# Norm roots on one core: square root, turned columns, reciprocal and spreading replaced by the exponential of a logarithm, in place in PSUM

## What is computed

```python
def rms_norm(x, g):
    xf = x.astype(jnp.float32)
    y = xf * lax.rsqrt(jnp.mean(xf * xf, axis=-1, keepdims=True) + EPS)
    return (y * g.astype(jnp.float32)).astype(x.dtype)

def layer_norm(x, g, b):
    xf = x.astype(jnp.float32)
    mu = jnp.mean(xf, axis=-1, keepdims=True)
    var = jnp.mean(jnp.square(xf - mu), axis=-1, keepdims=True)
    y = (xf - mu) * lax.rsqrt(var + LN_EPS) * g.astype(jnp.float32) + b.astype(jnp.float32)
    return y.astype(x.dtype)
```

## Time and profile before

| | us |
|---|---|
| median of 3 runs | 3126.02 (3125.41 to 3126.05) |
| the profiled execution | 3123.1 |
| its span, first to last instruction | 3121.3 |
| PE busy in it | 2922.6 (94%) |
| DVE busy | 1522.6 (49%) |
| ACT busy | 1160.0 (37%), of it 53 table loads 68.0 |
| POOL busy | 1310.3 (42%) |

### The profile page before, as it was taken

The page is one execution under the profiler, slowest core; times in us unless marked ns, Lnnn a source line. Parts: engine busy times, 40 slices in busy tenths (PEclk is TensorE's granted clock), DMA queues, the critical chain, the costliest instruction groups (busy, mean ns, idle before and its releaser), DMA issues.

```text
span 3121.3 us, 40174 instructions
## 1 busy us (share of the span) xinstructions
PE 2922.6 (94%) x15552; PEld 2150.9 (69%) x15552; DVE 1522.6 (49%) x2324; ACT 1160.0 (37%) x1827; POOL 1310.3 (42%) x798
## 2 busy tenths in 40 slices
PE   6999999999999999999999999998889979979997
PEld 4666557888888788888978888684564238546533
DVE  4765645563231545343341111556675655477665
ACT  4434424122111423333252222424434653453465
POOL 3644334454443435353445555457531024764200
PEclk9999999999999999999999999999999999989998
DMA  5310213444322112121123333220258932114695
GB/s 228 108 34 14 85 57 121 149 142 149 133 98 67 55 48 87 43 81 61 55 100 101 99 96 95 68 81 28 76 190 320 381 147 82 54 50 184 256 383 202
DMA packets 85884, 375.12 MB, mean 120 GB/s; under 512 B 9408, under 2 KB 11968, under 8 KB 76608
## 3 DMA queue, kind: packets, MB, share of 16 engines
q1 hardware_dynamic: 68416, 310.41, 28.5%
q10 hardware_dynamic: 12672, 45.37, 3.7%
q0 software_dynamic: 4608, 16.78, 1.4%
HBM read 557.07 MB, written 29.36 MB: 188 GB/s over the span
## 4 chain that ended last, share of the span: by engine, by line
PE 78%; DVE 11%; DMA 3%; ACT 3%; issue 2%; POOL 1%; SPq 0%; DVEq 0%; ACTq 0%; POOLq 0%
PE PS L105 77%; DVE SCR L120 2%; DMA ALL<-in_moe 2%; DVE SM L135 1%; PE PS L108 1%; DMA BF<-in_ada 1%; DVE SCR L132 1%; DVE SCR L126 1%; DVE SM L120 1%; DVE XF L126 1%; ACT SCR L114 1%; ACT RT L114 1%; DVE RTX L126 1%; DVE RTX L117 0%; DVE SM L123 0%
## 5 line engine op out<-in xcount | busy, mean ns | idle before, releaser
L105 PE MATMUL PS<-RT,WH 128*128 128x512 f32 (+1 forms) x5696 | 1518.5, 369 | 34.4 <-ACT SCR L114 9.4
L105 PEld LDWEIGHTS PS<-RT,WH 128*128 128x128 f32 x5696 | 1030.8, 190 | 271.2 <-issue 31.7
L120 POOL TENSOR_TENSOR WL<-RAW,WH 128x1024 fp32r<-128x1024 f32 x284 | 703.0, 2478 | 765.7 <-ACT WH L114 765.5
L105 PE MATMUL PS<-RT,WL 128*128 128x512 f32 (+1 forms) x2848 | 926.0, 366 | 0.0
L105 PEld LDWEIGHTS PS<-RT,WL 128*128 128x128 f32 x2848 | 493.2, 191 | 56.8
L114 ACT ACTIVATE WH<-RAW 128x1024 fp32r<-128x1024 f32 x284 | 298.4, 1054 | 602.4 <-PE PS L105 533.6
L120 POOL TENSOR_TENSOR RT<-SCR,RT 128x512 fp32r<-128x512 f32 (+2 forms) x174 | 222.6, 1287 | 406.3 <-ACT RT L114 314.3
L120 DVE TENSOR_TENSOR SCR<-PS,SCR 128x512 f32<-128x512 f32 (+1 forms) x106 | 58.8, 571 | 483.9 <-PE PS L105 465.9
L105 PE MATMUL PS<-ALL,SCR 128*32 x576 | 268.2, 610 | 24.4 <-DVE SCR L120 13.8
L105 PE MATMUL PS<-RTX,SCR 128*32 128x512 f32 x1152 | 268.4, 617 | 0.0
L126 DVE SCALAR_TENSOR_TENSOR XF<-PS,SM,XF 128x512 f32<-128x512 f32 x240 | 149.7, 658 | 216.3 <-PE PS L105 215.7
(11 more groups left out here) (238 smaller groups left out, 3639.9 us busy)
## 6 DMA issues: line engine op xcount, KB each, us to landing
ALL<-in_moe SPq DMA_DIRECT2D x100, 2048.0 KB, 8.4
ALL<-in_moe SPq DMA_DIRECT2D x100, 1024.0 KB, 14.0
RAW<-in_ff SPq DMA_DIRECT2D x132, 512.0 KB, 3.6
BF<-in_ada SPq DMA_DIRECT2D x64, 512.0 KB, 4.7
RAW<-in_ret SPq DMA_DIRECT2D x64, 512.0 KB, 3.5
RAW<-in_win SPq DMA_DIRECT2D x28, 512.0 KB, 3.5
RTX<-in_ada SPq DMA_DIRECT2D x26, 512.0 KB, 4.8
XF<-placed_in ACTq DMA_DIRECT2D x24, 512.0 KB, 8.7
```

Source lines behind the costliest of these rows:

```text
L105: return NOTHING if self.e is None else self.e.matmul(o, w, x, start=first, stop=last)
L120: return NOTHING if self.e is None else self.e.tensor_tensor(*a)
```

## The change

Four things are done:

- `act_root` computes ln(mean + eps) and then exp(-0.5 * that), both from the mean's bank in PSUM into the same bank. With it go the square root in SBUF, the turning, the columns' reciprocal and the spreading on PE and DVE; `dve_norm` reads the mean's bank, waits for ACT in place of PE, and the bank is given back by the last `dve_norm` (k = 7), not by `act_root`.
- Each two-part norm takes four banks fewer from the ring, each one-part norm two fewer. At the start four takes named "passed" keep the numbering of what follows.
- The retention's norm does the same in `RR` (SBUF), without the DVE reciprocal.
- `act_table` names Ln where it named Sqrt. Other square roots (attention heads, filters, token norms) stay.

```diff
         def act_root(act, s, j, n, eps):
-            r = sq_ring.take(("rr", s, j))[:, 0:n]
-            for count in sq_ring.empty(("rr", s, j)):
-                act.wait_ge(*count)
+            o = bank.of(("mean", s, j))[:, 0:n]
             act.wait_ge(*pe_done.at(("mean", s, j)))
-            act.activation(r, bank.of(("mean", s, j))[:, 0:n], ACT.Sqrt, bias=eps).then_inc(*act_done.done(("rr", s, j)))
-            bank.give(("mean", s, j), act_done.now())
-
-        def dve_root(dve, s, j, n):
-            r = bank.of(("rt", s, j))[:, 0:n].rearrange("p (c t) -> p c t", t=P)[:, :, 0]
-            dve.wait_ge(*pe_done.at(("rt", s, j)))
-            dve.reciprocal(root_column(j, n), r).then_inc(*dve_done.done(("rr", s, j)))
-            bank.give(("rt", s, j), dve_done.now())
+            act.activation(o, o, ACT.Ln, bias=eps).then_inc(*act_done.done())
+            act.wait_ge(*act_done.now())
+            act.activation(o, o, ACT.Exp, scale=-0.5).then_inc(*act_done.done(("rr", s, j)))
...
         def dve_norm(dve, s, k, j, n, A, B, *counts):
...
-            r = bank.of(("rb", s, j))[:, 0:n]
-            dve.wait_ge(*pe_done.at(("rb", s, j)))
+            r = bank.of(("mean", s, j))[:, 0:n]
+            dve.wait_ge(*act_done.at(("rr", s, j)))
             dve.scalar_tensor_tensor(h, XS[j][:, k, :], A[:, k:k + 1], r, ALU.mult, ALU.mult).then_inc(
                 *dve_done.done(("h", s, k, j)))
             if k == 7:
-                bank.give(("rb", s, j), dve_done.now())
+                bank.give(("mean", s, j), dve_done.now())
...
         def rms_pe(pe, s, parts):
             for j, _, n in parts:
                 pe_mean(pe, s, j, n)
-            if s != "att":
-                pe_roots(pe, s, parts)
...
                 if m == 11:
                     rms_pe(pe, "att", XP)
-            pe_roots(pe, "att", XP)
+            for n in range(4):
+                take_bank(pe, ("passed", n))
+                bank.give(("passed", n))
...
                 act.wait_ge(*pe_done.at(("rvar", h)))
-                act.activation(RR, bank.of(("rvar", h)), ACT.Sqrt, bias=EPS6).then_inc(*act_done.done(("rroot", h)))
+                act.activation(RR, bank.of(("rvar", h)), ACT.Ln, bias=EPS6).then_inc(*act_done.done())
                 bank.give(("rvar", h), act_done.now())
+                act.wait_ge(*act_done.now())
+                act.activation(RR, RR, ACT.Exp, scale=-0.5).then_inc(*act_done.done(("rroot", h)))
...
                 dve.wait_ge(*act_done.at(("rroot", h)))
-                dve.reciprocal(RR, RR).then_inc(*dve_done.done())
-                own()
                 for e in range(4):
```

More of the change, by code:

```diff
@@ L573, in pe_mean @@
             sq_ring.give(("sq", s, 7, j), pe_done.now())
[L575 to L600, removed]
         h_ring = ring([scr(0), scr(1), scr(2), scr(3)])
@@ L685, in rms_dve @@
         def rms_dve(dve, s, parts, A, B, before):
-            for j, _, n in parts:
-                dve_root(dve, s, j, n)
             free_h(dve, before)
@@ L858, in dve_ada @@
                     dve_add(dve, "att", k, j, n)
-            for j, _, n in XP:
-                dve_root(dve, "att", j, n)
             for b in range(2):
@@ L1410, in act_att @@
                             act_fold(act, g, blk)
-            act_table(act, ACT.Sqrt)
+            act_table(act, ACT.Ln)
             for g, m in OUT_LATE:
@@ L2119, in pe_variance @@
                 sq_ring.give(("sq", s, k, 0), pe_done.now())
-            pe_roots(pe, s, [(0, 0, S)])
         def act_layer_norm(act, s, b, before):
-            act_table(act, ACT.Sqrt)
+            act_table(act, ACT.Ln)
             for k in range(8):
@@ L2136, in dve_layer_norm @@
             bank.give(("mu", s), dve_done.now())
-            dve_root(dve, s, 0, S)
             free_h(dve, before)
```

## The result

The changed kernel takes 3149.69 us (median of 4 runs, 3147.0 to 3152.16) against 3125.72 (3122.55 to 3126.05) for the kernel before, run beside it: ratio 1.0077, 95% interval 1.0064 to 1.0091. It is slower by 24.0 us, where 18.8 was forecast. The profiled execution took 3151.77, its span is 3149.3.

What follows compares the result with a forecast made beforehand. PE, 78% of the chain, was taken to bound the kernel, norms counting only where it waits. Terms 11.15 + 2.06 + 2.85 + 2.1 + 1.04 - 0.45 = +18.75 us on 3126.02 gave 3144.8, range 3135 to 3152.

Steps and rivals of the forecast that it cites:

- Start: First norm: PE waits for the last normalization because the means' banks are held; +12.25 less 1.1, sum +11.15 us.
- "ff0": Two-part feed-forward norm: chain of 5.99 us on ACT ahead of `act_norm` shifts PE's start by +2.06 us.
- "ret": Retention's two-part norm: `act_norm` +2.85 us later, plus 2.1 for PE restarting at half clock.
- the credit of 1.1 for the clock: Start: PE's slow restart was to lose 2.1 us instead of 3.2, so -1.1.
- give or take 1: Clock at "ff0" and other already slow restarts: drawn anew, zero net, within 1 us each.
- One-part norms: Four norms ("ff1", "ln0", "ln1" twice): chain 2.62 instead of 2.36 us, +0.26 each, +1.04 together.
- Head 3: Last retention head: first product at 1578.7 instead of 1579.15, -0.45 us, bounds -1.5 and +1.9.
- hidden: Load ahead of the attention heads' first root: covered by 2.33 us of ACT idle time; uncovered it would cost 1.28.
- A: Rival: the late start is made up because something other than PE bounds attention; +9.6, 3135.6 us; chance 0.08.
- B: Rival: not slower, loads between Ln and Exp don't hold ACT; +2.4, 3128.4 us; chance 0.04.
- C: Rival: a load after a root costs twice its row, over 14 loads; +18, 3162.8 us; chance 0.05.
- D: Rival: first norms start as before, POOL not catching DVE, clock kinder; 3141 to 3143 us; 0.80 together with the forecast.

Runs made afterwards that it cites:

- the second group of runs: The changed kernel run again unaltered, with more rounds, for a second trace and firmer median: 3153.13 us (4 runs).
- e12: Changed kernel with two unread one-column memsets added among DVE's first instructions: 3152.2 us (5 runs).
- e10: Changed kernel with the two places of the first norm's roots put back in the ring of the squares' tiles: 3149.14 us (4 runs).
- e11: Kernel before with one more place taken in the ring of the squares' tiles behind the first norm: 3126.28 us (10 runs).
- e2: Kernel before with only the start's two mean banks given back late, by the last normalization: 3134.66 us (10 runs), ratio 1.0029.
- e1: Changed kernel with the four passed banks taken ahead of the start's means: 3140.67 us (4 runs), ratio 1.0044.
- e7: Changed kernel with 24 unread transposes behind the means of every RMS norm but the first: 3148.26 us (5 runs).
- e8: Changed kernel with passed banks ahead of the means, logarithms ahead of exponentials, 24 unread transposes, and the squares' ring as before: 3130.29 us (10 runs), ratio 1.0014.

## Why the prediction was right or wrong, step by step

- **Direction and mechanism** were right: slower, PE's wait at each norm, three loads in a row ahead of `act_norm`, the largest part of the loss a bank held at the start (8 to 10 of the 25 us). The Trainium skill, "ScalarE: Activation LUTs", section "What ACT_TABLE_LOAD costs", has a load of 1283 ns, which the trace repeats, and a drain of 1380 ns with it, which it doesn't: Ln ends at 32.43, the load begins at 32.45, Exp at 33.75. The size is another matter: by the table of stretches the forecast of 18.75 was 4.2 short. The start was 1.3 too small, "ff0" 2.6, and the three stretches that held only small terms or none 1.9 together; "ret" was 1.5 too large. That the time still fell inside the range is in part the luck of this one error against the others, and the second group of runs lies 1.1 us outside it.
- **Start, forecast +12.25 - 1.1 = +11.15.** First norm forecast at 41.5 and PE at 54.85; e12 has PE at 54.75 and e10 at 54.51. The wait was exact, the credit of 1.1 for the clock was mis-sized: from PE's first projection matmul to the mark at 112.34 it is 69.0 to 69.8 us with the old norms and 68.3 to 69.3 with the new, 0.5 in the mean. And one thing was missed. The means may run slowly, which the old norms hide but for 0.7 us and the new ones don't (56.85): 2.1 more, in two of four traces (I take the slow means for PE at half clock, which their lengths suggest, 1.22 and 1.06 as under a granted 0.50 ahead of "ff0", and the clock column doesn't show). Stretch by stretch: +12.4.
- **"ff0", forecast +2.06, measured +4.6.** The chain that was added up holds: Ln to `act_norm` is 5.91 (forecast 5.99). Set stretch by stretch, the 4.6 are 1.5 from the mark to the root, 2.4 from the root to PE's restart and 0.7 behind it. The 1.5 are what the sum had at nothing: DVE's addition caught beside POOL. The 2.4 are 7.62 us against 5.65 in two of the five old-norm traces and 4.87 in the other three; the forecast was read from one of the two, where slow means already delay the old `act_norm` (3.93 us behind the root instead of 3.14), so it came out as 2.06. The 0.7 are the clock, which was counted as even: it falls behind the restart in each of the four traces of the new norms, and did so in two of five of the old. That part lies within the "give or take 1"; the part ahead of the root doesn't, and it is the step that failed.
- **"ret", forecast +2.85 + 2.1, measured +3.5.** The wait is +2.75 (7.62 against 4.87 in four of the old-norm traces, 5.53 in e11, so 2.6 in the mean). The clock did fall to 0.50, as foreseen, in every trace of the new norms; but what is left for it is 0.75 to 0.85, not 2.1. This error has the opposite sign of the one in "ff0".
- **One-part norms, forecast +0.26 each**: 22.64 against 22.48 us in "ln0"'s stretch, 33.85 against 33.63 in "ff1"'s, so +0.16 and +0.22. **Head 3, forecast -0.45**: 413.48 against 413.87, -0.39. The load ahead of the attention heads' first root is **hidden**, as said: at 78.18 ACT has it behind it and still waits 1.03 us for PE.
- **Rivals.** A fell with e2 and e1, B and C with the 1.31 us from the end of one activation to the start of the next. D is not seen in any trace of the change: DVE was caught beside POOL each time, and the first norm stands at 41.24 to 43.60.
- **The level.** Every term was read from one profiled execution, and it was a kind one: its means ran fast, its retention stretch is the shortest of five (132.03), and its last mark comes 1 to 9 us earlier than in the other traces with the old norms, once e2's 10 us are taken off. Its 2.9 us to the median were added back, but the terms kept its draws: fast means at the start, and in "ff0" the opposite, a fallen clock (568.94, the second longest of five) that made the term for the wait small.

The sum of granted clock short of 1.00, over stretches of 1 us from 62 us on, is 79 to 90 us in the five old-norm traces and 91 to 99 in the four new ones: about 13 more. At most that much of the loss is clock. By the stretches about 4 us are left for it: 23.0 less 12.4 (start), 1.5 and 2.4 ("ff0", to the root and from it to PE), 2.6 ("ret") and 0.4 (the one-part norms less head 3). Where in the last stretch it falls differs from trace to trace; whether the changed kernel draws more falls there or had worse luck is open.

## What to carry over

Before replacing a chain of small steps with fewer larger ones, list what the steps held and gave back. Here a result written over its own input kept two PSUM banks busy for the length of a stage, and that cost some four times as much as the new roots added at any one norm. Ln and Exp alternating on ACT paid a table load at each turn here, so group by function, not by part. Take more than one trace of the kernel before if the terms are as small as a clock draw: two draws differ by more than most of the terms of this sum.

## What the runs showed of the hardware

- Logarithm and exponential each wanted a table of their own: a load of 1.28 us stood between them every time, 14 such loads on the path.
- Writing a logarithm over its own PSUM input cost no more than writing it to SBUF (662 ns, against 670 in the retention heads, 512 columns each).
- A DVE operation that read two tensors in SBUF and started behind a wide one of POOL lasted until POOL was done: 8 columns took 2.31 us and ended with POOL, an addition of 256 columns took 2.38 in place of 0.42 and ended 0.28 after it. One that started 0.05 us ahead of POOL wasn't held. Not every DVE operation was: in the changed kernel a reciprocal of 256 columns takes 1.75 us wholly beside POOL's subtraction (at 200.87) and 1.75 with POOL idle (at 206.06).
- A pause of 0.46 us stays at one place in DVE's instruction stream, whatever tile or semaphore is named there (nine traces; with two instructions added in front, e12, it stands one row earlier).
- PE's clock column can read 1.00 while eight matmuls take 4.66 us in place of 2.85, at the start of the program; there only the lengths tell.
- 24 transposes ahead of a wait of 4.17 us put the clock's fall off by about 1 us and didn't prevent it (e7); ahead of a wait of 2.3 us no fall came at "ff0", and one about 1 us late at "ret" (e8).
